# ScalarE gates two expert slots at a time in a retrieval layer

## The chip, the cores and the metric

The kernel runs on one core of one Trainium2 chip. The metric is the device time of one execution in microseconds (us). A core has five engines with an instruction queue each: TensorE (PE, matrix products), VectorE (DVE), ScalarE (ACT), GpSimd (POOL) and SyncE (SP). Each runs its queue in order and waits on semaphores; 16 DMA engines move data beside them. All arithmetic is in float32.

## The reference, cut to what matters

Two layers of a backbone over 256 latent tokens and 256 context tokens. Each layer has a mixer (pooling, attention, a matrix memory) and then a feed-forward part by expert retrieval, which is where the change lies. Layer 0 does it for both streams (512 tokens), layer 1 for the latent one (256 tokens).

```
for a block of 128 tokens:
    q = (hb @ w_q).reshape(P, PEER_HEADS, 2, PEER_DKEY // 2)
    s = einsum('phcd,hcnd->phcn', q, subkeys)
    ... top 16 of each half, top 16 of their sums: expert index, best (8 heads x 16)
    g = softmax(best)
    a = gelu(einsum('pd,phkd->phk', hb, u_tab[expert]), approximate=False)
    y = einsum('phk,phkd->pd', g * a, v_tab[expert])
```

So each token has 128 chosen experts. For each of them a row of u_tab (1024 numbers) is dotted with the token, the Gelu of the dot is multiplied by the gate g, and the row of v_tab is added with that weight.

## The kernel before

**Tiles and slots.** The feed-forward part runs over tiles of 128 tokens, one token to a partition: four tiles in layer 0, two in layer 1. In each tile it takes 128 slots m, one after the other; slot m is the m-th chosen expert of all 128 tokens. 32 slots make a quad (QUAD), so a tile has four quads; Q counts quads in a layer and n is the slot in its quad. There are 512 + 256 = 768 slots in all.

**The way of one slot.** (1) GpSimd starts an indirect DMA (`gather`, L391) that fetches, for each token, one row of the joined table uv (1024 numbers of u, 1024 of v: 8 KB for a token, 1 MB for the slot) into one of 8 places of `ring` (in regA). It first waits until the slot 8 before has been used (`v_used`), because it takes its place. (2) VectorE waits for the landing and dots the u half with the tokens' rows (`dot`, L1111); the result is a column of `araw`. (3) ScalarE, in `gated`, takes the Gelu of that column (L734), multiplies it by the gate weight (L735) into a column of `coef`, and scales the 128x128 identity by it, which gives the diagonal matrix `diag` (L738, in sqreg, 8 of them, DIAGS). (4) TensorE multiplies this diagonal with the v half, two instructions of 512 columns, which the profile counts as four matmuls with four weight loads (`values`, L1526), and adds up in the accumulator `acc` (bank67); the last one increments `v_used`, which frees the place in the ring.

**What stands between.** TensorE's queue holds, for each n, first `aside(Q, n)` and then `values` of the slot two before (BEHIND = 2). `aside` has pieces of the next queries (L1474), their scores (L1493), transposes (L1506, L1516), and in the last tile of layer 0 pieces of the next layer's modulation (L1537, L1548). ScalarE's queue holds after `gated(Q, n)` what belongs to those: evacuation of queries at n = 7, 15, 23, 31 (L702), of scores at n = 1 and 17 (L715, L716), the hidden rows of the next tile at n = 6 of one quad (L722), the modulation rows (L449) and, after n = 27, the Exp for the next quad's gates (L726). Exp and Gelu need different tables, so two table loads stand around it. VectorE chooses experts of the coming quad between its dots.

**The end of a tile.** When all 128 slots of a tile have been added, ScalarE copies the accumulator to `yrow` (`sums_out`, L745). In its queue this stands behind `gated` of the slot n = 3 of the next tile. TensorE may not begin the next tile's first `values` before that (`y_ready`). The sums are then transposed (L1516) and added to the tokens by VectorE (L1120). After the last tile of a layer nothing stands between.

Of the kernel before, what the change touches and what calls it, by code (L numbers as in the profile page):

```python
# [18 lines left out]
ACT = mybir.ActivationFunctionType  # L19
# [46 lines left out]
DIAGS = 8  # L66
# [52 lines left out]
def build(nc, x_in, c_in, par_in, con_in, w_in, uq_in, ukv_in, pw_in, sk_in, uv_tabs, out):  # L119
    with ExitStack() as ctx:  # L120
# [6 lines left out]
        def signal(name, first, second=None):  # L127
            return Signal(ctx, nc, name, first, first if second is None else second)
# [26 lines left out]
        def shaped(reg, off, a, b=None, c=None):  # L155
            if b is None:
                return reg[:, off:off + a]
            if c is None:
                return reg[:, off:off + a * b].rearrange("p (a b) -> p a b", a=a)
            return reg[:, off:off + a * b * c].rearrange("p (a b c) -> p a b c", a=a, b=b)  # L160

        ring = shaped(regA, 0, RING, 2 * D)
        diag = shaped(sqreg, 0, DIAGS, P)
# [34 lines left out]
        araw = shaped(regB, 3664, 2, QUAD)  # L198
        gact = regB[:, 3728:3760]
        coef = regB[:, 3760:3792]  # L200
        bv = shaped(regB, 3792, 2, QUAD)
        wts = shaped(regB, 3856, 2, QUAD)
# [11 lines left out]
        ident = con[:, C_ID:C_ID + P]  # L214
# [101 lines left out]
        diag_ready = signal("diag_ready", SLOTS * NT[0], SLOTS * NT[1])  # L316
# [86 lines left out]
        def _(a):  # L403
            steps = [0]

            def link(ins):
                steps[0] += 1
                ins.then_inc(act_step, 1)
                a.wait_ge(act_step, steps[0])
# [55 lines left out]
            for l in range(DEPTH):  # L465
# [73 lines left out]
                for c in range(2):  # L539
                    a.wait_ge(pool_mm.sem, pool_mm.at(l, c + 1))  # L540
                    if c == 0:
                        a.wait_ge(in_mm.sem, in_mm.at(l, 21 if l == 0 else 19))
                    a.activation(hT[:, c, 0:c1], ps[4 + c][:, 0:c1], ACT.Copy,
                                 scale=par[:, l, PB_PS + c:PB_PS + c + 1]).then_inc(pool_out.sem, 1)
# [144 lines left out]
                for k in range(KC):  # L689
                    a.wait_ge(hx_ready.sem, hx_ready.at(l, KC + k + 1))  # L690
                    for s in streams[l]:
                        ins = a.activation(hT[:, k, s * SEQ:(s + 1) * SEQ], hT[:, k, s * SEQ:(s + 1) * SEQ], ACT.Identity,  # L692
                                           scale=A2[:, k, s:s + 1], bias=modT[:, 24 + k, s:s + 1])
# [34 lines left out]
                def gated(Q, n):  # L728

                    m = Q * QUAD + n  # L730
                    if n == 0:
                        a.wait_ge(w_ready.sem, w_ready.at(l, Q + 1))
                    a.wait_ge(dotted.sem, dotted.at(l, m + 1))
                    link(a.activation(gact[:, n:n + 1], araw[:, Q % 2, n:n + 1], ACT.Gelu))  # L734
                    link(a.activation(coef[:, n:n + 1], gact[:, n:n + 1], ACT.Copy, scale=wts[:, Q % 2, n:n + 1]))  # L735
                    if m >= DIAGS:
                        a.wait_ge(v_used.sem, v_used.at(l, m - DIAGS + 1))
                    a.activation(diag[:, m % DIAGS, :], ident, ACT.Copy, scale=coef[:, n:n + 1]).then_inc(diag_ready.sem, 1)  # L738

                def sums_out(i):  # L740
                    a.wait_ge(v_used.sem, v_used.at(l, (i + 1) * P))
# [17 lines left out]
                for Q in range(nq):  # L759
                    i, r = divmod(Q, QUADS)  # L760
                    now, late = queried(Q, nt), queried(Q - 1, nt)
                    if l == 0 and Q == 11:

                        a.wait_ge(psc_mm.sem, psc_mm.at(0, 2 * PH))
                        a.dma_start(uqw, uq_in[1]).then_inc(mixw, 16)
                        a.dma_start(poolw[:, :, :], pw_in[1]).then_inc(mixw, 16)
                    if l == 0 and Q == nq - 1:

                        a.wait_ge(top_done.sem, top_done.at(0, PH * nt))
                        a.dma_start(ukvw, ukv_in[1]).then_inc(mixw, 16)  # L770
                    for n in range(QUAD):
                        gated(Q, n)
                        if n == 1 and late is not None and Q:
                            keys(late + 1)
                        if n % 8 == 7 and now is not None:
                            query(now // PH, (2 * now + n // 8) % HC)
                        if n == 17 and now is not None:
                            keys(now)
                        if n == 3 and r == 0 and i:
                            sums_out(i - 1)  # L780
                        if n == 6 and r == 2 and i + 1 < nt:
                            rows_in(i + 1)
                        if l == 0 and i == 3 and n % 4 == 3 and n < 24:
                            ada_rows(1, 6 * r + n // 4, 6 * r + n // 4 + 1)
                        if n == 27 and Q + 1 < nq:
                            exponentials(Q + 1)
# [906 lines left out]
```

## Time and profile before

| | us |
|---|---|
| median of the runs | 2903.13 |
| lowest, highest of the three | 2894.71, 2903.93 |
| the profiled execution, device time | 2898.94 |
| its span in the trace, first to last instruction | 2897.1 |

| engine | busy us | share of the span |
|---|---|---|
| PE | 2395.5 | 83% |
| DVE | 1623.2 | 56% |
| ACT | 1064.6 | 37% |
| POOL | 851.8 | 29% |

The span begins with 505 us of layer 0's mixer and first choices, then come its 512 slots (to about 1905 us), layer 1's mixer (to about 2228 us), and its 256 slots. A row of the profile names the engine, the line of the kernel, the instruction and what is written and read; "idle before" is the time in which that engine stood still just before such instructions, with what released it. A matmul's end is modelled, so TensorE's busy share isn't its share of peak.

### The profile page before, as it was taken

The numbers are of one execution on the slowest core, as the hardware profiler recorded it, in microseconds if no ns is written. First come the engines' busy times: TensorE is split into PE (matmuls) and PEld (weight loads), VectorE is DVE, ScalarE is ACT, GpSimd is POOL, SyncE is SP. The second block draws the span as 40 slices with busy tenths as digits, with TensorE's granted clock in tenths as the row PEclk, the third lists the DMA queues.
The fourth block names the chain that finished last, engine by engine and source line by source line (L and its number), as shares of the span: only waits on it lengthen the run. The fifth ranks groups of instructions, "written<-read, shape, count | busy, mean of one in ns | idle before, by whom it ended". The sixth has DMA issues, their size and how long they took to land.

```text
span 2897.1 us, 24069 instructions
## 1 busy us (share of the span) xinstructions
PE 2395.5 (83%) x7312; PEld 1129.7 (39%) x7312; DVE 1623.2 (56%) x3861; ACT 1064.6 (37%) x3055; POOL 851.8 (29%) x796
## 2 busy tenths in 40 slices
PE   7988888998778799898777777779788998777777
PEld 3455654543223244443223222235457443232222
DVE  1043533766766666666666565332454677667764
ACT  2133422334343333444333333333431434333333
POOL 1000000434434443343443433310001444444442
PEclk9988879999999999999999999999789999999999
DMA  6233002999999999999999999922005999999998
GB/s 270 73 135 127 1 30 73 416 421 421 421 397 420 421 421 421 386 421 421 421 421 405 421 421 421 422 113 87 1 1 183 422 421 421 421 394 422 421 422 330
DMA packets 127314, 918.90 MB, mean 317 GB/s; under 512 B 14160, under 2 KB 15440, under 8 KB 15696
## 3 DMA queue, kind: packets, MB, share of 16 engines
q0 software_dynamic: 110592, 805.36, 67.0%
q1 hardware_dynamic: 15152, 102.69, 9.3%
q10 hardware_dynamic: 1440, 9.32, 0.8%
q8 instruction: 58, 0.95, 0.1%
q14 instruction: 72, 0.59, 0.1%
HBM read 916.25 MB, written 1.05 MB: 317 GB/s over the span
## 4 chain that ended last, share of the span: by engine, by line
DMA 48%; PE 35%; ACT 7%; DVE 6%; issue 3%; POOL 0%; SPq 0%; ACTq 0%; PEldq 0%; DVEq 0%; POOLq 0%
DMA regA<-uv_dram,idx 47%; PE bank L1526 12%; PE bank L1251 5%; PE bank L1449 3%; DVE regA L1111 3%; PE bank L1474 3%; PE bank L1261 1%; PE bank L1191 1%; ACT sqreg L738 1%; PE bank L1371 1%; PE bank L1407 1%; PE bank L1311 1%; PE bank L1351 1%; ACT regB L735 1%; PE bank L1314 1%
## 5 line engine op out<-in xcount | busy, mean ns | idle before, releaser
L1526 PE MATMUL bank<-regA,sqreg 128*128 128x512 f32 x3072 | 1509.8, 617 | 362.0 <-ACT sqreg L738 315.6
L391 POOL DMA_INDIRECT regA<-uv_dram,idx x768 | 829.2, 1080 | 1897.1 <-PE bank L1526 1119.4
L1111 DVE SCALAR_TENSOR_TENSOR regA<-regA,regB 128x1024 f32<-128x1024 f32 x768 | 940.8, 1225 | 696.6 <-DMA regA<-uv_dram,idx 695.7
L1526 PEld LDWEIGHTS bank<-regA,sqreg 128*128 128x128 f32 x3072 | 535.6, 190 | 1166.7 <-ACT sqreg L738 725.5
L734 ACT ACTIVATE regB<-regB 128x1 f32<-128x1 f32 x768 | 155.7, 203 | 1176.1 <-DVE regA L1111 1167.1
L738 ACT ACTIVATE sqreg<-con,regB 128x128 f32<-128x128 f32 x768 | 308.2, 401 | 25.2
L735 ACT ACTIVATE regB<-regB 128x1 f32<-128x1 f32 x768 | 226.1, 294 | 25.0
L1474 PE MATMUL bank<-hT,wring 128*128 128x256 f32 x768 | 214.5, 388 | 11.3 <-ACT hT L692 11.3
L1474 PEld LDWEIGHTS bank<-hT,wring 128*128 128x128 f32 x768 | 147.7, 195 | 141.1 <-issue 130.9
L1251 PE MATMUL bank<-hT,wring 128*128 128x512 f32 (+2 forms) x384 | 148.7, 545 | 15.5 <-ACT hT L431 12.4
L1251 PEld LDWEIGHTS bank<-hT,wring 128*128 128x128 f32 (+1 forms) x384 | 72.2, 193 | 91.2 <-issue 84.1
L839 DVE SCALAR_TENSOR_TENSOR regA<-regA 8x512 f32<-8x512 f32 x2 | 1.4, 680 | 163.9 <-ACT regA L512 163.9
L1449 PE MATMUL bank<-hT,wring 128*128 128x512 f32 (+1 forms) x256 | 89.6, 511 | 3.3 <-PE bank L1449 1.8
L611 ACT ACTIVATE regA<-bank,asm 128x512 f32<-128x512 f32 (+1 forms) x48 | 29.5, 615 | 104.8 <-DVE asm L910 103.9
L1449 PEld LDWEIGHTS bank<-hT,wring 128*128 128x128 f32 x256 | 50.8, 201 | 41.6 <-issue 37.7
L1111 DVE DVE_READ_ACCUMULATOR regA<-regA,regB 128x1 f32 x768 | 63.2, 82 | 0.0
L1004 DVE SCALAR_TENSOR_TENSOR xT<-bank,modT,xT 128x256 f32<-128x256 f32 x24 | 10.9, 481 | 85.8 <-PE bank L1449 85.8
L1371 PE MATMUL bank<-regA 128*64 128x128 f32 x320 | 53.5, 318 | 6.6 <-DVE hT L922 6.5
L1351 PE MATMUL bank<-regA 96*128 96x512 f32 (+1 forms) x96 | 57.6, 692 | 0.7 <-ACT regA L587 0.7
L878 DVE TENSOR_REDUCE rowss<-regA 128x16 f32<-128x1536 f32 (+1 forms) x8 | 12.4, 1553 | 78.4 <-ACT regA L572 78.4
L1261 PE MATMUL bank<-wring,hT 128*128 128x256 f32 x224 | 49.6, 381 | 1.2 <-PE bank L1251 0.6
L1371 PEld LDWEIGHTS bank<-regA 128*64 128x64 f32 x320 | 40.3, 158 | 17.1 <-issue 17.1
(207 smaller groups left out, 1788.7 us busy)
## 6 DMA issues: line engine op xcount, KB each, us to landing
wring<-w_dram SPq DMA_DIRECT2D x96, 1024.0 KB
regA<-uv_dram,idx POOLq DMA_INDIRECT x768
mlaw<-uq_dram ACTq DMA_DIRECT2D x2, 1152.0 KB, 9.7
xT<-x_dram ACTq DMA_DIRECT2D x1, 2048.0 KB, 12.1
mlaw<-ukv_dram ACTq DMA_DIRECT2D x2, 1024.0 KB, 11.8
subk<-sk_dram ACTq DMA_DIRECT2D x2, 1024.0 KB, 4.8
out_dram<-xT SPq DMA_DIRECT2D x1, 1024.0 KB, 4.8
con<-con_dram SPq DMA_DIRECT2D x1, 938.0 KB, 5.1
```

The costliest lines, as they stand in the source:

```text
L391: g.indirect_dma_start(ring[:, s, :], None, uv_tabs[l], bass.IndirectOffsetOnAxis(idx[:, i % 2, k:k + 1], 0)).then_inc(landed[s], 16)
L734: link(a.activation(gact[:, n:n + 1], araw[:, Q % 2, n:n + 1], ACT.Gelu))
L735: link(a.activation(coef[:, n:n + 1], gact[:, n:n + 1], ACT.Copy, scale=wts[:, Q % 2, n:n + 1]))
L738: a.activation(diag[:, m % DIAGS, :], ident, ACT.Copy, scale=coef[:, n:n + 1]).then_inc(diag_ready.sem, 1)
L1111: v.scalar_tensor_tensor(out=ring[:, s, 0:D], in0=ring[:, s, 0:D], scalar=1.0, in1=hrow[:, i % 2, :], op0=ALU.mult, op1=ALU.mult, accum_ou ...
L1251: mm = p.matmul(dst[0:m, 0:n], wt[:, k, o:o + m], hT[:, k, 0:n], start=(k == 0), stop=(k == KC - 1))
L1261: mm = p.matmul(dst[:, 0:WT], hT[:, k, t * P:(t + 1) * P], wt[:, k, :], start=(k == 0), stop=(k == KC - 1))
L1351: p.matmul(ps[i % 2][:, k0:COLS], qT[0:QK, h, t * P:(t + 1) * P], kT[0:QK, h, k0:COLS], start=True, stop=True).then_inc(sc_mm.sem, 1)
L1371: mm = p.matmul(ps[3][64 * f:64 * f + 64, 0:P], vrow[:, j, h * VD:(h + 1) * VD], pt[:, i % 2, j, :], start=(j == js[0]), stop=(j == 3))
L1449: mm = p.matmul(ps[4 + b % 2][:, 0:c1], wt[:, k, (b % 2) * P:(b % 2 + 1) * P], hT[:, k, 0:c1], start=(k == 0), stop=(k == KC - 1))
L1474: mm = p.matmul(ps[q % 2][:, 0:SEQ], wt[:, k, (q % 2) * P:(q % 2 + 1) * P], hT[:, k, s * SEQ:(s + 1) * SEQ], start=(k == 0), stop=(k == KC ...
L1526: mm = p.matmul(acc[:, f * 512:f * 512 + 512], diag[:, m % DIAGS, :], ring[:, s, D + f * 512:D + f * 512 + 512], start=(m % P == 0), stop= ...
```

## The change

`gated` does nothing for an even n. For an odd n it waits for that slot's dot (which comes after the even one's), takes the Gelu of both columns in one instruction, makes the two products one behind the other with one wait behind the second, waits once until both places of `diag` are free, and writes the two diagonals. The code that calls `gated` is as before, so what stands behind an odd n stands behind the pair, and what stands behind the even n = 6 (the hidden rows, L722) now stands ahead of the pair 6 and 7.

```
                     if n == 0:
                         a.wait_ge(w_ready.sem, w_ready.at(l, Q + 1))
+                    if n % 2 == 0:
+                        return
                     a.wait_ge(dotted.sem, dotted.at(l, m + 1))
-                    link(a.activation(gact[:, n:n + 1], araw[:, Q % 2, n:n + 1], ACT.Gelu))
+                    link(a.activation(gact[:, n - 1:n + 1], araw[:, Q % 2, n - 1:n + 1], ACT.Gelu))
+                    a.activation(coef[:, n - 1:n], gact[:, n - 1:n], ACT.Copy, scale=wts[:, Q % 2, n - 1:n])
                     link(a.activation(coef[:, n:n + 1], gact[:, n:n + 1], ACT.Copy, scale=wts[:, Q % 2, n:n + 1]))
                     if m >= DIAGS:
                         a.wait_ge(v_used.sem, v_used.at(l, m - DIAGS + 1))
-                    a.activation(diag[:, m % DIAGS, :], ident, ACT.Copy, scale=coef[:, n:n + 1]).then_inc(diag_ready.sem, 1)
+                    for j in (n - 1, n):
+                        a.activation(diag[:, (m - n + j) % DIAGS, :], ident, ACT.Copy, scale=coef[:, j:j + 1]).then_inc(diag_ready.sem, 1)
```

Lines behind this move down by four: L745 becomes L749, L1111 becomes L1115, L1526 becomes L1530. The queues of the other engines hold the same instructions in the same order.

ScalarE's queue at the start of a second tile, before: slots n = 2 and 3, the copy of the old tile's sums (from bank67), and slot n = 4.

```order
L734 ACTIVATE regB<-regB 128x1
L735 ACTIVATE regB<-regB 128x1
L738 ACTIVATE sqreg<-con,regB 128x128
L734 ACTIVATE regB<-regB 128x1
L735 ACTIVATE regB<-regB 128x1
L738 ACTIVATE sqreg<-con,regB 128x128
L745 ACTIVATE regB<-bank67 128x1024
L734 ACTIVATE regB<-regB 128x1
```

The same place now:

```order
L736 ACTIVATE regB<-regB 128x2
L737 ACTIVATE regB<-regB 128x1
L738 ACTIVATE regB<-regB 128x1
L742 ACTIVATE sqreg<-con,regB 128x128 x2
L749 ACTIVATE regB<-bank67 128x1024
L736 ACTIVATE regB<-regB 128x2
```

Six instructions of slots 2 and 3 have become five (the last row holds two), both diagonals stand last, and the copy follows them.

ScalarE's queue at the end of a layer, before: the last two slots and the copy of the last sums.

```order
L734 ACTIVATE regB<-regB 128x1
L735 ACTIVATE regB<-regB 128x1
L738 ACTIVATE sqreg<-con,regB 128x128
L734 ACTIVATE regB<-regB 128x1
L735 ACTIVATE regB<-regB 128x1
L738 ACTIVATE sqreg<-con,regB 128x128
L745 ACTIVATE regB<-bank67 128x1024
```

And now:

```order
L738 ACTIVATE regB<-regB 128x1
L742 ACTIVATE sqreg<-con,regB 128x128 x2
L736 ACTIVATE regB<-regB 128x2
L737 ACTIVATE regB<-regB 128x1
L738 ACTIVATE regB<-regB 128x1
L742 ACTIVATE sqreg<-con,regB 128x128 x2
L749 ACTIVATE regB<-bank67 128x1024
```

The diagonal of the last slot but one, which stood ahead of the last slot's Gelu, now stands behind it and both products.

## Rows read from the trace of the kernel before

**Rows 1.** The page: the chain that ended last, by line.

```profile
DMA regA<-uv_dram,idx 47%; PE bank L1526 12%; PE bank L1251 5%; PE bank L1449 3%; DVE regA L1111 3%; PE bank L1474 3%; PE bank L1261 1%; PE bank L1191 1%; ACT sqreg L738 1%; PE bank L1371 1%; PE bank L1407 1%; PE bank L1311 1%; PE bank L1351 1%; ACT regB L735 1%; PE bank L1314 1%
```

**Rows 2.** Windows: busy PE, PEld, DVE, ACT, POOL (count), clock, DMA share, GB/s.

```profile
560.00:840.00 280.00, 236.62 (x563) 95.66 (x561) 187.57 (x457) 110.72 (x347) 110.63 (x109) 1.00 1.01 421
...
2650.00:2860.00 210.00, 164.62 (x334) 56.38 (x332) 133.46 (x306) 80.96 (x258) 85.99 (x84) 1.00 1.01 421
```

**Rows 3.** Timelines of the four engines (start, length, [idle before]): one slot.

```profile
966.74 1.23 DVE L1111 SCALAR_TENSOR_TENSOR regA<-regA,regB 128x1024 f32<-128x1024 f32 x1 [1.25 <-DMA regA<-uv_dram,idx]
...
968.00 0.20 ACT L734 ACTIVATE regB<-regB 128x1 f32<-128x1 f32 x1 [1.52 <-DVE regA L1111]
968.24 0.29 ACT L735 ACTIVATE regB<-regB 128x1 f32<-128x1 f32 x1
968.56 0.40 ACT L738 ACTIVATE sqreg<-con,regB 128x128 f32<-128x128 f32 x1
...
969.02 1.98 PE L1526 MATMUL bank<-regA,sqreg 128*128 128x512 f32 x4 [0.50 <-ACT sqreg L738]
...
971.27 0.94 POOL L391 DMA_INDIRECT regA<-uv_dram,idx  x1 [1.55 <-PE bank L1526]
```

**Rows 4.** Line L391 up to 834.5, line L1111 up to 849.5, from 505.

```profile
L391 POOL DMA_INDIRECT regA<-uv_dram,idx x129: 932/939/1983, 505.2 to 833.9; - x129
...
L1111 DVE SCALAR_TENSOR_TENSOR regA<-regA,regB x129: 1211/1225/1247, 514.3 to 848.8; 128x1024 f32<-128x1024 f32 x129
```

**Rows 5.** The same lines up to 1198.5 and 1204.

```profile
L391 POOL DMA_INDIRECT regA<-uv_dram,idx x265: 932/939/1986, 505.2 to 1198.0; - x133
...
L1111 DVE SCALAR_TENSOR_TENSOR regA<-regA,regB x265: 1205/1225/1247, 514.3 to 1203.5; 128x1024 f32<-128x1024 f32 x133
```

**Rows 6.** Timeline of ACT: two slots that stood ready, layer 0's start.

```profile
525.65 0.40 ACT L738 ACTIVATE sqreg<-con,regB 128x128 f32<-128x128 f32 x1
525.96 0.19 ACT L734 ACTIVATE regB<-regB 128x1 f32<-128x1 f32 x1
```

**Rows 7.** Timeline of PE around 842: two slots at a stretch.

```profile
842.38 3.70 PE L1526 MATMUL bank<-regA,sqreg 128*128 128x512 f32 x8 [1.83 <-ACT sqreg L738]
```

**Rows 8.** Start of the second tile: timelines of ACT, PE and POOL.

```profile
858.29 1.00 ACT L745 ACTIVATE regB<-bank 128x1024 f32<-128x1024 f32 x1
...
859.35 12.39 PE L1526 MATMUL bank<-regA,sqreg 128*128 128x512 f32 x24 [8.87 <-ACT regB L745]
...
863.40 0.94 POOL L391 DMA_INDIRECT regA<-uv_dram,idx  x1 [11.71 <-PE bank L1526]
```

**Rows 9.** Windows at the start of each layer's second tile.

```profile
860.00:864.00 4.00, 4.00 (x7) 1.61 (x6) 3.56 (x10) 1.70 (x6) 0.60 (x1) 0.62 0.44 184
...
2576.00:2580.00 4.00, 4.00 (x10) 1.75 (x9) 3.57 (x12) 1.61 (x6) 1.87 (x2) 0.93 0.45 127
```

**Rows 10.** ACT and POOL: slot 9's diagonal, slot 8's return, second tile.

```profile
874.71 0.40 ACT L738 ACTIVATE sqreg<-con,regB 128x128 f32<-128x128 f32 x1
...
878.54 1.35 POOL L391 DMA_INDIRECT regA<-uv_dram,idx  x1 [1.14 <-PE bank L1526]
```

**Rows 11.** Timelines of ACT and PE at the end of layer 1.

```profile
2884.52 0.40 ACT L738 ACTIVATE sqreg<-con,regB 128x128 f32<-128x128 f32 x1
2887.00 1.02 ACT L745 ACTIVATE regB<-bank 128x1024 f32<-128x1024 f32 x1 [2.07 <-PE bank L1526]
...
2884.98 1.98 PE L1526 MATMUL bank<-regA,sqreg 128*128 128x512 f32 x4 [0.47 <-ACT sqreg L738]
```

**Rows 12.** PE at the first slots of layer 0, and a window.

```profile
525.25 3.61 PE L1526 MATMUL bank<-regA,sqreg 128*128 128x512 f32 x4 [3.27 <-ACT sqreg L738]
...
528.00:532.00 4.00, 4.00 (x12) 2.21 (x11) 2.95 (x9) 1.61 (x6) 1.65 (x2) 0.93 1.02 426
```

**Rows 13.** Timeline of ACT around an Exp.

```profile
1002.82 1.28 ACT L734 ACT_TABLE_LOAD   x1
1004.11 0.20 ACT L734 ACTIVATE regB<-regB 128x1 f32<-128x1 f32 x1
```

## The prediction

> **What bounds the kernel now.** I read the chain that ended last first: the gathers hold 47% of it and the value matmuls (L1526) 12%, while the ScalarE lines of a slot have about 1% each [rows 1]. The windows say why: through whole stretches of slots the DMA engines are 1.01 busy at 421 GB/s, with ScalarE busy 110.72 of 280 us and TensorE 236.62 [rows 2]. There a slot lasts as long as its data takes, 1.049 MB by 421 GB/s = 2.49 us (2.61 as the mean of the first tile, 334.5 us over 128 slots [rows 4], since other transfers come between), and no computing engine sets the pace. So what counts is when a place of the ring comes back, and whether transfers are still queued by then.
>
> The timelines give the way of one slot [rows 3]: dot from 966.74, Gelu 968.00, product 968.24, diagonal 968.56, matmuls 969.02, and the gather that takes the freed place at 971.27, 4.53 us after the dot began. Against that stands the time a gather has in the queue: the 129th begins at 833.9 and its dot at 848.8 [rows 4], 14.9 us, six slots' time. That is slack. The shortest such time I find is at a restart, where hardly anything is queued: the 265th gather at 1198.0, its dot at 1203.5 [rows 5], 5.5 us. So a return may come some 9 us later before data is missed.
>
> It is missed at the start of each tile but a layer's first, four times in all. TensorE stands still for 8.87 us until the copy of the sums (L745) at 858.29 is done, the gathers stand still for 11.71 us, and the DMA share falls to 0.44 in one window and to 0.45 in that of layer 1 [rows 8, 9]. That copy stands in ScalarE's queue behind slot n = 3. There, and at the last slot of each layer, ScalarE is on the path.
>
> **The change part by part.** *Removed:* 384 Gelu instructions at 0.20 us and 384 waits of the 768 behind Gelus. It is some 77 us of ScalarE's 1064.6 busy, all beside DMA work, so worth nothing where the DMA engines are full.
>
> *Inside a pair.* I count from the start of the odd slot's dot. The Gelu comes at 1.26 as before and the first product at 1.50 [rows 3]. Two instructions with no wait between overlap by 0.09: 0.31 from start to start where the first lasts 0.40 [rows 6]. So the second product starts 0.20 after the first, the first diagonal at 1.82 + 0.20 = 2.02 and the second at 2.33, where the odd slot's diagonal used to start at 1.82. The odd diagonal is 0.51 later. The even one waits for the odd dot as well, 2.49 + 0.20 = 2.69 later. TensorE then finds two slots ready, which it does in 3.70 us, 1.98 for the first and 1.72 more for the second [rows 3, 7]. Returns: the even slot's at 2.02 + 2.71 = 4.73 (2.71 is 971.27 less 968.56 [rows 3]), which is 7.22 after its own dot, 2.69 later than now; the odd one's at 6.45, 1.92 later.
>
> *In the full stretches.* 2.69 of some 9 us of slack is used. Price 0. Were the cover gone, up to 2.69 us for each of 384 pairs would show. GpSimd's two gathers of a pair then come 1.72 us apart at 0.94 us each, which fits.
>
> *At the four tile starts.* The copy follows the odd diagonal of n = 3, so it, TensorE's first values and all the gathers behind come 0.51 later, and as the DMA engines are dry there this shows in full: 4 x 0.51 = 2.0 us. Below nothing I see no reason. Upwards: while TensorE catches up, the pairs' lateness must hide behind its backlog. Slot 8 of the second tile shows it: its place is returned at 878.54, hence its matmuls began at about 876.6; the new pair's diagonal would start 0.71 after slot 9's of now (0.20 by the pair and 0.51 by the shift), at 875.42 [rows 10] and be done by 875.8. Covered by 0.8 us, and later slots have more transfers queued. If it weren't, 2.69 each.
>
> *At the two layer ends.* No transfer is behind the last slot. Now its diagonal starts at 2884.52, its matmuls at 2884.98, the copy at 2887.00 [rows 11]. With the pair, the first diagonal starts 0.20 later, its matmuls at 2885.18, and both slots' take 3.70, to 2888.88, where they ended at 2886.96: 1.92 us later. In layer 0 the next mixer waits for it just so: 2 x 1.92 = 3.8 us.
>
> *At the two layer starts* the first dots stand ready, TensorE begins at 525.25 at half clock, and the DMA share there is 1.02 [rows 12]: the 0.20 us more is hidden behind the eight transfers that are under way.
>
> *What stands behind odd slots.* Evacuations of queries and scores and the Exp come 0.51 us later, the hidden rows (n = 6) earlier. TensorE asks for them a slot or more later and VectorE's gates for the Exp three slots later: price 0, and if it showed, 0.51 for each, in stretches where 9 us are in hand. The two table loads around an Exp end with the Gelu at 1004.11, which the second load alone keeps for 1.28 us [rows 13]; the pair behind n = 27 waits for n = 29 anyway and hides that.
>
> Sum: 0 + 2.0 + 3.8 = 5.9 us on the profiled execution's 2898.94, or 2904.8. The median shown is 2903.13, which gives 2909.0. The profiled execution is a run like the three, so I take the middle, 2907.
>
> **TensorE's clock.** With pairs it works 3.70 us and rests 4.98 - 3.70 = 1.28, where it rested 0.50 [rows 3]. After 1.83 us of rest eight matmuls still took 3.70 (full, 2.4 GHz [rows 7]); after 3.27 us of rest four took 3.61, half clock, 1.2 GHz [rows 12]. So 1.28 is on the good side. The Trainium skill (TensorE: Matmul & The Clock Gate, HAM oscillation — how this bites in real kernels) warns of just this pattern: bursts of matmuls shorter than the waits between them each begin at the low clock, and work should be issued so that the engine stays busy. By that rule the change would be a loss (below); by the rows it isn't.
>
> **The rivals.** *A, as summed:* 2907, between 2901 and 2911 with the spread of the runs.
>
> *B, the backlog doesn't cover the pairs at the tile starts:* with few transfers queued the even slot's return is late by 2.69 once in each of the four restarts, 4 x 2.69 = 10.8 more: 2918. It decides by whether slot 9's diagonal comes before TensorE is through with slot 7. For it: the cover is only 0.8 us. Against: slot 8 alone is so near, the later ones have more.
>
> *C, slower, the clock falls between pairs:* in quads without queries (twelve of 24, 192 pairs) a pair's matmuls would take 6.9 us at half clock, twice 3.44, against 4.98 of data. It decides at a rest somewhere between 1.83 and 3.27 us. Then TensorE would be the bound: even if only the first slot of a burst were slow (3.61 + 1.72 = 5.33), that is 0.35 x 192 = 67 us: 2974. Against: the rest of 1.28, and an engine that never rests gets its clock back. By the page's rule it would come out so; rows 7 speak against it.
>
> *D, the ends are hidden too:* if the 0.51 and the 1.92 overlap something that I don't see, 2901.
>
> *E, faster:* if Gelus that are late behind an Exp hold up the ring today, 24 x 1.28 = 31 us would be won: 2876. Against: the DMA share is 1.01 across such stretches [rows 2].
>
> **How the numbers follow.** A 0.68, B 0.15, C 0.04, D 0.09, E 0.04. Range: A and D with B's 2918 as the upper end, and 2899 below. 0.3% is 8.7 us, about what a measurement of this kernel tells from no change: 2894.4 to 2911.8. Within it lie D and nearly all of A (0.74); slower are B, C and A's edge (0.21); faster is E with a little of D (0.05).
>
> **What would show it.** In the new profile: ScalarE busy near 985 us; one Gelu for a pair, the diagonals 0.31 apart, TensorE in bursts of eight matmuls of 3.70 us with rests near 1.3; gathers in twos 1.72 apart; the DMA share 1.01 in the same stretches, so 2.49 us a slot; the copies at the tile starts 0.5 us later after the fourth dot; the last copy of a layer 3.9 us after the start of the last diagonal, where it was 2.48. Wrong would be: a DMA share under 1 inside a tile, bursts longer than 3.7, or a restart gap in the gathers that grew by more than 0.6 us.

## The result and the profile after

The changed kernel takes 2910.66 us (median of 20 runs, 2902.11 to 2914.24) against 2903.85 for the kernel before (20 runs, 2894.71 to 2910.48): a ratio of 1.0023, 95% interval 1.0015 to 1.0030, or 6.8 us more. That is within 0.3%, where the forecast lay: it had 5.9 us more, and 2907 as the time, because it stood between two starting points. One disturbed execution of the kernel copy0_single, of 6447.8 us, is left out of its numbers below.

The full stretches first, as windows (length, busy us of PE, PEld, DVE, ACT and POOL with counts, clock, DMA share, GB/s):

```profile
560.00:840.00 280.00, 228.92 (x573) 103.57 (x572) 188.74 (x464) 87.69 (x295) 113.28 (x109) 0.98 1.01 421
...
1560.00:1900.00 340.00, 265.41 (x880) 105.15 (x878) 181.96 (x417) 91.39 (x311) 125.40 (x113) 0.93 1.01 421
2650.00:2860.00 210.00, 155.18 (x336) 60.12 (x335) 136.30 (x317) 62.84 (x215) 85.28 (x84) 1.00 1.01 421
```

Against [rows 2] ScalarE has 87.69 us of 280 where it had 110.72, and the DMA engines are as full as before, 1.01 at 421 GB/s. So the work that was saved there is worth nothing, and the lateness of the pairs costs nothing there. One thing is new: the clock of the second row, the last tile of layer 0, is 0.93 (and 0.98 in the first row). Before it was 1.00:

```profile
1560.00:1900.00 340.00, 254.19 (x863) 96.58 (x862) 182.96 (x418) 115.06 (x368) 120.39 (x109) 1.00 1.01 418
```

A pair, from the timelines of DVE, ACT, PE and POOL (start, length, [idle before]); it answers to [rows 3]:

```profile
970.29 1.22 DVE L1115 SCALAR_TENSOR_TENSOR regA<-regA,regB 128x1024 f32<-128x1024 f32 x1 [1.26 <-DMA regA<-uv_dram,idx]
...
971.55 0.20 ACT L736 ACTIVATE regB<-regB 128x2 f32<-128x2 f32 x1 [3.53 <-DVE regA L1115]
971.79 0.29 ACT L737 ACTIVATE regB<-regB 128x1 f32<-128x1 f32 x1
971.99 0.28 ACT L738 ACTIVATE regB<-regB 128x1 f32<-128x1 f32 x1
972.30 0.69 ACT L742 ACTIVATE sqreg<-con,regB 128x128 f32<-128x128 f32 x2
...
972.75 3.70 PE L1530 MATMUL bank<-regA,sqreg 128*128 128x512 f32 x8 [1.27 <-ACT sqreg L742]
...
975.01 0.94 POOL L391 DMA_INDIRECT regA<-uv_dram,idx  x1 [2.32 <-PE bank L1530]
976.73 0.94 POOL L391 DMA_INDIRECT regA<-uv_dram,idx  x1 [0.78 <-PE bank L1530]
```

The Gelu starts 1.26 us after the odd dot began, the second product 0.20 after the first, the diagonals at 2.01 (forecast 2.02), TensorE rests 1.27 (1.28) and takes 3.70 for two slots, and the two gathers come 4.72 and 6.44 us after the odd dot's start (4.73 and 6.45), 1.72 apart. One sign did not come as forecast: ScalarE was to be busy near 985 us and is busy 904.1 (31% of the span). The forecast counted the Gelus alone, 77 us. The lines of a slot fall from 155.7, 226.1 and 308.2 us (Gelu, product, diagonal) to 78.2, 220.3 and 266.3, and the two products also overlap by 0.09 us in each of 384 pairs, for 160.5 us in all. It is worth nothing here, like the 77.

The start of the second tile, timelines of ACT, PE and POOL, which answers to [rows 8]:

```profile
863.79 0.69 ACT L742 ACTIVATE sqreg<-con,regB 128x128 f32<-128x128 f32 x2
864.39 1.00 ACT L749 ACTIVATE regB<-bank 128x1024 f32<-128x1024 f32 x1
...
865.45 13.54 PE L1530 MATMUL bank<-regA,sqreg 128*128 128x512 f32 x24 [7.44 <-ACT regB L749]
...
869.50 1.71 POOL L391 DMA_INDIRECT regA<-uv_dram,idx  x1 [10.28 <-PE bank L1530]
872.39 1.28 POOL L391 DMA_INDIRECT regA<-uv_dram,idx  x1 [1.18 <-PE bank L1530]
```

The copy starts 2.61 us after the dot of slot 3 began, where it was 2.14: 0.47 later. But then the first six slots take 13.54 us where they took 12.39 [rows 8]: the second gather comes 2.89 us after the first. TensorE came back to full clock later than in the profile before. Two windows of this kernel, in the second tile of each layer and as far behind the start of the copy as those of [rows 9] (1.71 and 4.29 us):

```profile
866.10:870.10 4.00, 4.00 (x6) 1.55 (x5) 3.61 (x9) 1.38 (x5) 0.60 (x1) 0.50 0.41 172
...
2585.41:2589.41 4.00, 4.00 (x7) 1.60 (x6) 3.71 (x10) 0.73 (x3) 1.91 (x2) 0.63 0.25 51
```

The clock is 0.50 and 0.63 where it was 0.62 and 0.93, the DMA share 0.41 and 0.25 where it was 0.44 and 0.45.

The end of layer 1, ACT and PE, for [rows 11]:

```profile
2894.59 0.69 ACT L742 ACTIVATE sqreg<-con,regB 128x128 f32<-128x128 f32 x2
2898.78 1.02 ACT L749 ACTIVATE regB<-bank 128x1024 f32<-128x1024 f32 x1 [3.50 <-PE bank L1530]
...
2895.05 3.70 PE L1530 MATMUL bank<-regA,sqreg 128*128 128x512 f32 x8 [1.18 <-ACT sqreg L742]
```

From the start of the last dot to the copy it is 6.20 us where it was 4.31 (2882.69 to 2887.00), in layer 0 6.21 against 4.30: 3.8 us in all, the 3.8 of the forecast.

The two profiled spans differ by 11.8 us (2908.9 and 2897.1), more than the medians. Counted from the starts of the dots, the difference is made up of 5.9 before the first dot, where nothing was changed, 4.5 between the first and the last dots of the two layers, 3.8 at the layer ends, and 2.5 us less in layer 1's mixer, unchanged too. So before a cause was named for the 4.5, the unchanged parts had to be told from the rest. All tables below count from dots.

### The profile page after: what moved, and what is told of

Same layout as the page of the kernel before. It is cut to its first block, busy times and chain, and to the rows that moved or that the text cites. A ratio compares the mean times of both kernels' runs of the same rounds, so it can differ in the third digit from the quotient of the medians.

```text
span 2908.9 us, 23309 instructions
## 1 busy us (share of the span) xinstructions
PE 2373.7 (82%) x7312; PEld 1172.3 (40%) x7312; DVE 1625.3 (56%) x3861; ACT 904.1 (31%) x2671; POOL 840.5 (29%) x796
## 4 chain that ended last, share of the span: by engine, by line
PE 42%; DMA 41%; ACT 7%; DVE 6%; issue 3%; POOL 0%; SPq 0%; ACTq 0%; POOLq 0%; PEldq 0%; DVEq 0%
DMA regA<-uv_dram,idx 41%; PE bank L1530 17%; PE bank L1255 5%; DVE regA L1115 3%; PE bank L1478 3%; PE bank L1453 3%; PE bank L1265 1%; PE bank L1375 1%; ACT sqreg L742 1%; PE bank L1195 1%; PE bank L1355 1%; PE bank L1411 1%; PE bank L1315 1%; ACT regB L738 1%; PE bank L1318 1%
## 5 line engine op out<-in xcount | busy, mean ns | idle before, releaser
L1530 PE MATMUL bank<-regA,sqreg 128*128 128x512 f32 x3072 | 1493.8, 623 | 402.7 <-ACT sqreg L742 371.6
L391 POOL DMA_INDIRECT regA<-uv_dram,idx x768 | 818.0, 1065 | 1918.4 <-PE bank L1530 1173.4
L1115 DVE SCALAR_TENSOR_TENSOR regA<-regA,regB 128x1024 f32<-128x1024 f32 x768 | 941.2, 1226 | 698.1 <-DMA regA<-uv_dram,idx 696.7
L1530 PEld LDWEIGHTS bank<-regA,sqreg 128*128 128x128 f32 x3072 | 571.2, 195 | 1138.6 <-ACT sqreg L742 577.1
L736 ACT ACTIVATE regB<-regB 128x2 f32<-128x2 f32 x384 | 78.2, 204 | 1365.0 <-DVE regA L1115 1365.0
L742 ACT ACTIVATE sqreg<-con,regB 128x128 f32<-128x128 f32 x768 | 266.3, 394 | 12.5
L1478 PE MATMUL bank<-hT,wring 128*128 128x256 f32 x768 | 216.3, 391 | 11.5 <-ACT hT L692 11.5
L1255 PE MATMUL bank<-hT,wring 128*128 128x512 f32 (+2 forms) x384 | 149.2, 547 | 15.4 <-ACT hT L431 12.4
L737 ACT ACTIVATE regB<-regB 128x1 f32<-128x1 f32 x384 | 113.2, 295 | 12.7
L738 ACT ACTIVATE regB<-regB 128x1 f32<-128x1 f32 x384 | 107.1, 279 | 0.0
L1115 DVE DVE_READ_ACCUMULATOR regA<-regA,regB 128x1 f32 x768 | 63.1, 82 | 0.0
L882 DVE TENSOR_REDUCE rowss<-regA 128x16 f32<-128x1536 f32 (+1 forms) x8 | 12.4, 1553 | 75.9 <-ACT regA L572 75.9
```

What stands on the lines that cost most here:

```text
L391: g.indirect_dma_start(ring[:, s, :], None, uv_tabs[l], bass.IndirectOffsetOnAxis(idx[:, i % 2, k:k + 1], 0)).then_inc(landed[s], 16)
L737: a.activation(coef[:, n - 1:n], gact[:, n - 1:n], ACT.Copy, scale=wts[:, Q % 2, n - 1:n])
L742: a.activation(diag[:, (m - n + j) % DIAGS, :], ident, ACT.Copy, scale=coef[:, j:j + 1]).then_inc(diag_ready.sem, 1)
L1115: v.scalar_tensor_tensor(out=ring[:, s, 0:D], in0=ring[:, s, 0:D], scalar=1.0, in1=hrow[:, i % 2, :], op0=ALU.mult, op1=ALU.mult, accum_ou ...
L1255: mm = p.matmul(dst[0:m, 0:n], wt[:, k, o:o + m], hT[:, k, 0:n], start=(k == 0), stop=(k == KC - 1))
L1478: mm = p.matmul(ps[q % 2][:, 0:SEQ], wt[:, k, (q % 2) * P:(q % 2 + 1) * P], hT[:, k, s * SEQ:(s + 1) * SEQ], start=(k == 0), stop=(k == KC ...
```

## The experiments

Two theories stood against each other. Theory 1: pairs cost only where no transfer is queued, at the layer ends and the starts of the later tiles (restarts, below). Theory 2: they cost something in every stretch. Two medians of the changed kernel differ by 5 us (2910.7 and 2905.4), so each kernel's profile was also taken apart. "Restarts" is the sum over the four later tiles of the time from the start of the dot 8 slots ahead of the tile to that 40 slots into it. "Other slots" is what is left of both layers from the ninth dot on. "Ends" is last dot to last copy, both layers. A ratio is against runs of the kernel before from the same series (medians 2903.1 to 2904.0) and is estimated from all runs of both, so it isn't the quotient of two medians.

| kernel | restarts | other slots | ends | median, ratio, 95% interval |
|---|---|---|---|---|
| before | 514.1 | 1471.4 | 8.6 | 2903 to 2904 |
| before_again | 512.6 | 1473.2 | 8.6 | one run, 2902.9 |
| after | 518.9 | 1472.1 | 12.4 | 2910.7, 1.0023 (1.0015 to 1.0030) |
| after_again | 515.7 | 1472.1 | 12.4 | 2905.4, 1.0017 (1.0003 to 1.0031) |
| undo_end | 518.2 | 1471.7 | 9.5 | 2909.4, 1.0015 (1.0001 to 1.0029) |
| undo_start | 514.8 | 1471.2 | 12.4 | 2907.9, 1.0011 (0.9997 to 1.0025) |
| undo_both | 515.4 | 1469.7 | 9.6 | 2905.1, 1.0010 (0.9996 to 1.0024) |
| copy1_single | 509.7 | 1471.6 | 8.6 | 2900.2, 0.9991 (0.9977 to 1.0004) |
| copy0_single | 509.7 | 1471.5 | 8.6 | 2900.2, 0.9990 (0.9979 to 1.0002) |
| copy1_pair | 509.7 | 1472.7 | 12.4 | 2902.9, 0.9997 (0.9983 to 1.0011) |
| warm_single | 510.1 | 1472.2 | 8.6 | 2898.6, 0.9994 (0.9979 to 1.0009) |
| warm_pair | 510.7 | 1472.7 | 12.4 | 2905.9, 1.0009 (0.9996 to 1.0021) |
| group4 | 548.0 | 1593.7 | 20.0 | 3062.8, 1.0536 (1.0508 to 1.0565) |

**The same kernels again.**

> The changed kernel itself, for a second profile: 1.0023. If the clock's return in the restarts is set by the program, the matmuls of the first six slots of the second tile take 13.5 us again, and so do those of layer 1's second tile; if it is chance, they lie anywhere between 12.4 and 14.

> The kernel before, for a second profile. The 5.9 us by which the changed kernel's slots began later are in a part that the change doesn't touch. If that is chance, this profile's first dot starts anywhere between 510 and 522 us, and the slots of layer 0 take 1386 to 1387 us from there as before; if the kernel before always starts at 514, the change has an effect ahead of the slots.

Measured: 1.0017 for the changed kernel. Its first dot starts at 510.4 us, where its first profile had 520.2; the kernel before had 514.3 and 514.2. Over all profiles it lies between 510.4 and 521.5, and in those without pairs between 514.3 and 520.5, in no order with the change, so the 5.9 us ahead of the slots are put down to chance (the two profiles of the kernel before agree, so a small part that isn't can't be excluded). The clock's return varies too: in the second profile of the same kernel the first six slots of the second tile took 12.01 us, not 13.54.

```profile
856.23 12.01 PE L1530 MATMUL bank<-regA,sqreg 128*128 128x512 f32 x24 [7.45 <-ACT regB L749]
...
859.93 0.94 POOL L391 DMA_INDIRECT regA<-uv_dram,idx  x1 [9.94 <-PE bank L1530]
861.64 0.94 POOL L391 DMA_INDIRECT regA<-uv_dram,idx  x1 [0.78 <-PE bank L1530]
```

The timelines of PE and POOL of after_again: after the same rest (7.45 against 7.44) the second gather is 1.71 us behind the first, and not 2.89.

**One part undone.** Slots that meet a condition are gated as before:

```
+                    if Q and Q % QUADS == 0 and n < 4:          # undo_start
+                    if Q == QUADS * nt - 1 and n >= QUAD - 2:   # undo_end; undo_both: either
+                        ... the lines of the kernel before, for this slot ...
+                        return
                     if n % 2 == 0:
                         return
```

> The changed kernel, with the first four slots of each later tile gated one at a time; all others in pairs, those of the tile's end too. Theory 1: the copy of the sums comes 0.48 us earlier four times, 1.9 us, so about 1.0016. If TensorE's later return to full clock in the changed kernel (0.2 to 1.2 us later in each of the four restarts) hangs on the place of the copy, another 3.4 us come back, 1.0005. Theory 2: 1.0023. In the profile the matmuls of the first six slots of the second tile take 12.4 us if the clock returns as in the kernel before, 13.5 if as in the changed one.

> The changed kernel, with the last two slots of each layer gated one at a time as before; all other slots in pairs. Theory 1 (the cost sits where nothing is queued behind): it wins back 2 x 1.92 = 3.8 us of the 6.8, so about 1.0010 of the kernel before, and each layer's last copy starts 2.48 us after the start of the last diagonal again (3.9 in pairs). Theory 2 (the cost is spread over the full stretches): nothing is won back, 1.0023.

> Both: the first four slots of each later tile and the last two of each layer one at a time, the other 734 of 768 or so in pairs. Theory 1: 1.000, or up to 1.0012 if the clock's later return stays. Theory 2: 1.0022, since nearly all slots are still in pairs.

By the medians alone these four can hardly be told apart: 1.0017, 1.0015, 1.0011, 1.0010 for the changed kernel, the end undone, the start undone, both, each with 0.0014 to either side. The order is that of theory 1, no more. The table says more. The other slots, nearly all in pairs, take 1469.7 to 1472.1 whatever is undone, and 1471.4 and 1473.2 without any pair, so theory 2 is out, down to the 2 to 3 us by which these sums scatter. The restarts are less sharp: with the starts undone they take 514.8 and 515.4 us, with 512.6 and 514.1 in the kernel before, and in the three profiles with pairs there 515.7 to 518.9. The two profiles of the changed kernel alone are 3.2 us apart. In undo_start the first six slots of the second tile took 13.46 us with the copy back in its old place, so the clock's later return doesn't hang on that place. A shorter stretch separates them: from the start of slot 3's dot to that of slot 8, the first whose transfer had to wait for the copy, summed over the four restarts. Beside it stands how many of the four first gathers took 1.70 us or more, and not 0.94:

| kernel | slots 3 to 8, us | long first gathers |
|---|---|---|
| before, before_again | 51.0, 50.7 | 0, 0 |
| undo_start, undo_both | 51.0, 51.5 | 0, 0 |
| after, undo_end | 56.2, 56.1 | 4, 4 |
| after_again | 54.0 | 2 |

The dots beside these gathers say what goes on (timelines of DVE, in the order before, after, after_again; their first gathers start at 863.40, 869.50 and 859.93):

```profile
863.56 1.22 DVE L1111 SCALAR_TENSOR_TENSOR regA<-regA,regB 128x1024 f32<-128x1024 f32 x1
...
869.17 1.23 DVE L1115 SCALAR_TENSOR_TENSOR regA<-regA,regB 128x1024 f32<-128x1024 f32 x1
...
859.99 1.23 DVE L1115 SCALAR_TENSOR_TENSOR regA<-regA,regB 128x1024 f32<-128x1024 f32 x1
```

In the kernel before the first gather begins 0.16 us ahead of a dot and takes 0.94 us. The pairs bring the copy, and so the gather, 0.48 later; it now begins 0.33 us inside the dot, takes 1.71 us, and its transfer is dotted 6.28 us after its start where it was 5.57. In after_again TensorE was back at full clock sooner, the gather began 4.75 us behind the copy and not 5.11, again 0.06 us ahead of the dot, and took 0.94 us. Of the 752 gathers of the kernel before that wait for a place, 185 of the 214 that begin during a dot take over 1.0 us, and 5 of the other 538 do. Why they take longer the profile doesn't say. So a pair costs a restart its 0.48 us and, where the gather falls into the dot, some 0.8 us more.

With the end undone the ends take 9.5 us and not 8.6: I expected 3.8 us back and got 2.9. The timeline of PE of undo_end says why; the last single slots stand behind the last pair's eight matmuls, in one burst of sixteen:

```profile
2890.47 7.13 PE L1538 MATMUL bank<-regA,sqreg 128*128 128x512 f32 x16 [1.28 <-ACT sqreg L750]
```

**How far the slack reaches.** Four slots at a time:

```
-                    if n % 2 == 0:
+                    if n % 4 != 3:
                         return
+                    k0 = n - 3
...
+                    for j in range(k0, n):
+                        a.activation(coef[:, j:j + 1], gact[:, j:j + 1], ACT.Copy, scale=wts[:, Q % 2, j:j + 1])
...
-                    for j in (n - 1, n):
+                    for j in range(k0, n + 1):
```

> Four slots instead of two: one Gelu, four products, one wait, four diagonals. It doubles what a pair adds. The first slot's return comes 3 x 2.49 + 3 x 0.20 = 8.1 us late, against a slack worked out as some 9 us. Theory 1 (slack holds, cost where nothing is queued): DMA share still 1.01 inside the tiles, a layer's end 3 x 1.72 + 0.6 = 5.8 us later than in the kernel before, twice, a later tile's start 1.5 to 3 us later, four times: 11.5 + 6 to 12, about 1.007. Theory 2 (the slack is nearer to the pair's 2.7 than to 9): each of 192 groups loses several us, 1.2 or more, with a DMA share well under 1.

Measured: 3062.83 us, 1.0536 (1.0508 to 1.0565), 155 us and more than the kernel before. Neither total was right: the slack doesn't hold 8.1 us, and what each of 192 groups loses is 0.8 us, not several. The ends alone came out as expected, 11.4 us more (20.0 less 8.6) for 11.5; the other slots lost 122 us. The windows and the timelines of PE and POOL:

```profile
560.00:840.00 280.00, 225.39 (x558) 106.99 (x557) 175.88 (x437) 73.14 (x250) 122.21 (x103) 0.94 0.98 392
...
725.03 8.63 PE L1532 MATMUL bank<-regA,sqreg 128*128 128x512 f32 x16 [4.61 <-ACT sqreg L744]
...
728.79 0.94 POOL L391 DMA_INDIRECT regA<-uv_dram,idx  x1 [7.05 <-PE bank L1532]
```

The DMA engines move 392 GB/s where they moved 421. What I left out is that a group's lateness isn't 8.1 us alone. TensorE now rests 4.61 us, is at half clock for a part of the burst (sixteen matmuls take 8.63 us, and in undo_end 7.13), and works off four slots at once with queries and transposes between. From a first slot's dot to its return I count 12.5 to 16.1 us in this tile, where 4.53 + 8.1 = 12.6 was the sum. The queue falls to where a gather is dotted 5.8 us after it starts, near the 5.5 of [rows 5]. So the slack of some 9 us (14.9 less 5.5) isn't contradicted, and it was the lateness that I had too small: up to 16.1 less 4.53, 11.6 us. In the changed kernel the same counts give mostly 7.22 and 6.45 us, and from slot 24 of that tile on a gather's time in the queue is never under 11.3.

**Where the copy stands.**

```
-                        if n == 3 and r == 0 and i:
+                        if n == 1 and r == 0 and i:     # copy0_single: n == 0
                             sums_out(i - 1)
```

> The kernel before with the copy of a tile's sums behind slot n = 1 of the next tile instead of n = 3. If the four dry spells (DMA share 0.44 to 0.8 over some 10 us each, 3.3 us of transfer lost each) hang on the place of that copy alone, they all but go, 13 us: 0.9955. If they hang on TensorE's clock or on something else behind the copy, under 4 us.

> The changed kernel with the copy behind n = 1. Theory 1: the cost of pairs at the tile starts (1.9 to 4.5 us) goes with the dry spells, and only the two ends (3.8 us) are left against the kernel above: 0.9968. Theory 2 (pairs cost something inside the tiles): more than 1.0013 above the kernel above.

> The kernel before with the copy behind slot n = 0 of the next tile. It was behind n = 1 in an earlier run, 0.9991, where the dry spells were gone and the slots' stretches 4.9 us shorter, but TensorE still rested 3.9 us and fell to half clock. Behind n = 0 it rests some 2 us, so it should stay at full clock: the same 4.9 us or one or two more, 0.998 to 0.999. If TensorE's clock made part of the dry spells' cost, more.

Measured: 0.9991, 0.9997 and 0.9990, each with an interval that holds 1. The windows around the four restarts, of the kernel before and of copy1_single:

```profile
856.00:876.00 20.00, 16.65 (x41) 7.84 (x42) 14.75 (x36) 7.20 (x22) 7.21 (x7) 0.82 0.84 327
1190.00:1210.00 20.00, 15.94 (x45) 8.60 (x46) 15.15 (x39) 7.96 (x25) 6.75 (x6) 0.81 0.78 298
1526.00:1546.00 20.00, 16.11 (x52) 7.07 (x52) 13.41 (x34) 7.38 (x23) 5.22 (x6) 0.76 0.89 359
2570.00:2590.00 20.00, 17.23 (x42) 8.15 (x43) 15.08 (x38) 7.56 (x24) 7.31 (x8) 0.84 0.84 322
```
```profile
852.00:872.00 20.00, 16.10 (x38) 7.22 (x37) 16.57 (x49) 8.30 (x26) 8.17 (x7) 0.83 1.00 406
1190.00:1210.00 20.00, 20.00 (x58) 10.87 (x57) 16.30 (x42) 7.43 (x25) 10.68 (x8) 0.91 0.97 375
1526.00:1546.00 20.00, 20.00 (x82) 8.58 (x81) 13.64 (x33) 6.25 (x22) 8.35 (x8) 0.95 0.96 385
2570.00:2590.00 20.00, 19.91 (x46) 9.23 (x47) 16.48 (x43) 7.23 (x25) 9.32 (x8) 0.85 1.00 415
```

The dry spells have all but gone, shares of 0.96 to 1.00 for 0.78 to 0.89. In copy0_single the granted clock is 1.00 as well in all four such windows, and the restarts are no shorter for it (509.7). Yet the restarts got shorter by 2.9 to 4.4 us in all, and not by 13. I had counted the missing share as lost time; the dots show that a spell delays them by about 1 us each. Why so little comes back I haven't settled. With the copy early, pairs cost nothing at all at the restarts: 509.7 us with and without. What is left of their cost are the 3.8 us of the ends, and the medians differ by 2.7 (2902.9 and 2900.2). So the cost at the restarts did hang on the copy. Whether the two with single slots are faster than the kernel before, the medians don't settle: three or four us less each time.

**The clock in the restarts.** Eight matmuls of constants into an unused bank, ahead of TensorE's wait for the copy; their result isn't used:

```
                     if m % P == 0 and m:
+                        for _ in range(8):
+                            p.matmul(ps[3][:, 0:512], ident, con[:, 0:512], start=True, stop=True)
                         p.wait_ge(y_ready.sem, y_ready.at(l, m // P))
```

> The kernel before with eight added matmuls of 512 columns into an unused PSUM bank (identity times constants, the result is not used) at the head of each later tile, ahead of TensorE's wait for the copy: 16 of 0.43 us in the profile, 6.9 us, inside its rest of 8.9. If TensorE's half clock is what the first slots of a restart lose, the first gather follows the copy's start by 3.1 to 3.4 us instead of 5.1 and the second by 1.72 more in every restart: 2 us a restart at most, 0.9975 to 1.000.

> The same eight matmuls in the changed kernel. With the clock's chance taken out, the pairs should cost in a restart just the 0.48 us of the copy: its slots' stretches longer than those of the kernel above by 1.9 us in all (the profiles without these matmuls showed 1.7 to 4.5). If they are longer by 3 us or more again, the rest of the cost at the restarts isn't the clock.

Measured: 0.9994 and 1.0009. The timeline of PE in warm_pair, the added matmuls and the first six slots:

```profile
858.56 7.03 PE L1528 MATMUL bank<-con 128*128 128x512 f32 x16
866.16 10.57 PE L1532 MATMUL bank<-regA,sqreg 128*128 128x512 f32 x24 [0.57 <-ACT regB L749]
```

10.57 us at full clock for what took 12.39, 12.01 or 13.54 after a rest. The copy is as late as ever, but the first gather follows its start by 3.31 us (868.42 less 865.11) and not 5.11. That was expected of every restart and holds for three of the four in warm_pair and two in warm_single; in the others it is 3.90 to 4.52 us. The restarts take 510.1 and 510.7 us, nearly as short as with the early copy. So the dry spells' cost to the dots needs both the late copy and the half clock, and either remedy takes it away. The pair's part in it is then 0.6 us (510.7 less 510.1), not the 1.9 that I expected: the first gathers now begin 0.3 to 2.0 us ahead of the dot that they fell into before, and the copy's 0.48 us hardly shows in the dots. The medians of the two kernels differ by 7.4 us, more than the 0.6 and the 3.8 of the ends; single runs of warm_single lie between 2891.5 and 2909.4, so ten of each don't settle it.

## Why the prediction was right

**The bound, and 0 in the full stretches:** right. The other slots take 1472.1 us in both profiles of the changed kernel, 1471.4 and 1473.2 in the one before. The pair's own timetable came out to 0.01 us. ScalarE's saving was put at half of what it is (77 of 160.5 us), which costs the forecast nothing, since its price was 0 either way.

**The layer ends, 3.8:** right, 12.4 less 8.6, in every profile with a pair there.

**The tile starts, 2.0:** the mechanism was right, the term incomplete. The copy's shift was 0.47 of the 0.51 forecast, four times 1.9. What was left out is where the first gather then falls: inside a dot of VectorE in 10 of the 12 restarts with pairs, in none of the 16 without, and it then takes some 0.8 us longer. At slot 8 the three profiles with pairs there average 55.4 us and the four without 51.1, 4.4 more, for 1.9 by the shift and 2.6 by the longer gathers. Over the whole stretch of 48 slots they average 517.6 and 514.2: 3.4 more, with scatter of 3.2 us within one kernel, so that sum alone wouldn't exclude the 2.0. Whether pairs also make the clock's return later is open. "Below nothing I see no reason" was too strong: warm_pair shows 0.6, copy1_pair nothing. The forecast's sign of being wrong, a gap in the gathers grown by more than 0.6 us, must be read from the fourth dot to the first gather, 7.25 before and 7.73 after; GpSimd's idle time itself shrank from 11.71 to 10.28, since the last gather ahead of it comes later too.

**Sum:** 3.4 + 3.8 = 7.2 by the profiles, 6.8 by the medians (in the second series of the same kernel 1.0017, or 4.9), 5.9 forecast. That these lie so close together is in part luck: a tile-start term that was too small by 1.4 is within the scatter of either.

**Rival B** (the backlog doesn't cover the pairs) did not come about in the first slots: those with the nearest cover were returned with the shift of all others (in the second tile slot 8 is returned 7.24 us later on the profile's clock than in the kernel before, and slot 4 just as much). In the last tile of layer 0 slot 14 came back 7 us later than that shift, behind a rest of TensorE of 4.76 us, when four or more transfers were queued again.

**Rival C** did come about in part, where I hadn't looked, and no cost of it shows. The forecast's sign of it, bursts longer than 3.7 us, was there. I worked out the rest between bursts as 1.28 us from a stretch with 2.49 us a slot. In the last tile of layer 0 the other transfers stretch many slots, and the rest of a pair grows. The timeline of PE there:

```profile
1647.40 3.78 PE L1530 MATMUL bank<-regA,sqreg 128*128 128x512 f32 x4 [3.16 <-ACT sqreg L742]
1651.11 1.08 PE L1541 MATMUL bank<-wring,cS 128*32 128x256 f32 x8
```

After a rest of 3.16 us four matmuls take 3.78 us, half clock (1.2 GHz), as after the 3.27 us of [rows 12]. It is this that brings the window to 0.93, and it makes half of the whole kernel's fall from 0.961 to 0.944; the rest lies in the other tiles (0.95 for 0.99 in 1190:1526) and ahead of the slots. That a burst begins at the low clock after a wait, which the Trainium skill describes (TensorE: Matmul & The Clock Gate, HAM oscillation — how this bites in real kernels), shows in this tile. But its case has bursts shorter than the waits between them. The pair's 3.70 us of work and 1.28 of rest are not "just this pattern", as the forecast had it, and by that section it had no reason to expect rival C in the full stretches, where the clock was 0.98. The time stays, since the DMA share is 1.01 there and the slack takes up the two microseconds. In group4, where the slack is spent, the same effect is part of the price.

**Rivals D and E:** the ends were not hidden, and nothing of ScalarE's or the table loads' time came back.

## What to carry to other kernels

Where a queue of transfers sets the pace, as here, batching the small work of another engine won nothing inside the queue's stretch. It cost its full added latency at the ends, where nothing is queued behind. Where the pipeline is drained and started again it cost more than its latency, because the shift also moved a gather into VectorE's dot, and next to nothing once the copy was early or TensorE warm. Before batching, compare the time from a landing to the return of its buffer with the time a transfer spends queued, and add to the first what a longer rest of TensorE does to its clock and what side work stands in its queue. Where a step moves by half a microsecond, look at what it will then run beside. To see an effect of 0.1 to 0.3%, take the profile apart at the borders of what was changed: here unchanged parts moved by up to 11 us between profiles of kernels that are alike there.

## What the runs showed that I had not expected

A gather's instruction on GpSimd takes 0.94 us, but 1.70 to 1.99 in the restarts where it begins just behind the start of a dot on VectorE; a shift of 0.48 us made the difference. The time at which TensorE is back at full clock after a rest varies between profiles of one kernel: six slots took 13.54 and 12.01 us after the same 7.44 us of rest. A dry spell of the DMA engines with 3 us of missing share delayed the dots by about 1 us only. And a late copy costs nearly nothing if TensorE is kept busy meanwhile: 510.1 us for the restarts against 514.1 and 512.6.
